# A hybrid diffusion step: the expert slot table from one-hot products, and adaLN products in column groups

## What is computed

```python
# adaLN: per layer, for the context and the latent conditioning
mod = silu(c) @ w_ada[l] + b_ada[l]            # 1024 x 6144 weights
sh1, sc1, g1, sh2, sc2, g2 = split(mod, 6)
h  = rmsnorm(x, norm_g[0]) * (1 + sc1) + sh1   # then h @ w_in, mixers, @ w_out
x  = x + g1 * mix
h2 = rmsnorm(x, norm_g[1]) * (1 + sc2) + sh2
x  = x + g2 * moe(h2)

# MoE: sigmoid router, the best 4 of 8 groups, the best 8 of 64 experts for each token
scores = sigmoid(h2 @ w_router)
gates  = 2.5 * chosen / sum(chosen)            # 8 for each token
routed = sum_e gates_e * (silu(h2 @ w_gate[e]) * (h2 @ w_up[e])) @ w_down[e]
shared = (silu(h2 @ ws_gate) * (h2 @ ws_up)) @ ws_down
```

## Time and profile before

| | us |
|---|---|
| median of 3 runs | 1783.19 |
| lowest and highest | 1767.92 to 1783.76 |
| the profiled execution, its own time | 1778.72 |
| its span in the trace | 1776.5 |
| mean granted TensorE clock | 0.901 |

### The profile page before, as it was taken

How to read it: one execution, slowest core, us unless ns; L and a number is a source line. 1 busy time by engine, 2 the same in 40 slices (tenths; PEclk the granted TensorE clock), 3 DMA queues, 4 the chain that set the end, 5 groups by cost and what they waited for, 6 DMA issues and landing times. The chain is left out here.

```text
span 1776.5 us, 23526 instructions
## 1 busy us (share of the span) xinstructions
PE 1466.6 (83%) x8676; PEld 945.6 (53%) x8676; DVE 670.5 (38%) x1341; ACT 422.5 (24%) x797; POOL 318.5 (18%) x351
## 2 busy tenths in 40 slices
PE   5899978991999999998079998799649999999952
PEld 2478563950555555554026975566425555555521
DVE  2623567153222222222644337633512222222246
ACT  2333515120122222221033344321102211221201
POOL 2000000005223232321110000000243223223220
PEclk9899959995899999999589998799869999999975
DMA  8644102224699988885855322122159888889844
GB/s 282 221 142 148 69 36 83 95 83 180 226 339 349 338 327 329 298 316 177 347 189 203 122 101 95 39 95 95 57 208 365 312 310 331 318 305 336 315 192 166
DMA packets 127760, 379.22 MB, mean 213 GB/s; under 512 B 29824, under 2 KB 34752, under 8 KB 124448
## 3 DMA queue, kind: packets, MB, share of 16 engines
q1 hardware_dynamic: 86976, 291.31, 44.6%
q0 software_dynamic: 40672, 86.42, 13.5%
HBM read 480.47 MB, written 64.91 MB: 307 GB/s over the span
## 5 line engine op out<-in xcount | busy, mean ns | idle before, releaser
L1171 PE MATMUL bank<-slab,xT 128*64 128x256 f32 x2112 | 300.3, 396 | 21.3 <-issue 20.8
L1171 PEld LDWEIGHTS bank<-slab,xT 128*64 128x64 f32 x2112 | 180.9, 142 | 103.4 <-issue 36.9
L744 POOL DMA_INDIRECT sums_scratch<-h,table x112 | 112.8, 1007 | 539.3 <-PE bank L1157 437.4
L1840 DVE TENSOR_TENSOR work<-work,bank 128x128 f32<-128x128 f32 x112 | 32.3, 288 | 408.6 <-ACT work L1437 408.6
L1171 PE MATMUL bank<-ring,xT 128*64 128x256 f32 x960 | 150.2, 389 | 12.0 <-issue 12.0
L1186 PE MATMUL bank<-slab,work 128*64 128x512 f32 x528 | 147.4, 592 | 1.5 <-DVE work L1844 1.5
L828 PE MATMUL bank<-ring,scond 128*2 128x512 f32 x320 | 140.9, 598 | 1.0 <-issue 1.0
L1437 ACT ACTIVATE work<-bank 128x128 f32<-128x128 f32 x112 | 31.0, 277 | 456.8 <-PE bank L1171 456.8
L1518 DVE TENSOR_TENSOR w_lo<-ring,w_hi 128x2048 fp32r<-128x2048 f32 x32 | 72.9, 2291 | 157.2 <-ACT w_hi L1259 157.0
L1157 PE MATMUL bank<-consts,big 128*128 128x128 f32 x544 | 77.8, 288 | 65.2 <-DMA big<-rows_scratch,table 65.2
L1829 DVE COPY h<-bank 128x512 f32<-128x512 f32 x112 | 77.5, 692 | 127.2 <-PE bank L1186 127.2
(11 more groups left out here) (336 smaller groups left out, 2376.7 us busy)
## 6 DMA issues: line engine op xcount, KB each, us to landing
slab<-in_w_gate SPq DMA_DIRECT2D x112, 512.0 KB
slab<-in_w_up SPq DMA_DIRECT2D x112, 512.0 KB
slab<-in_w_down SPq DMA_DIRECT2D x112, 512.0 KB
ring<-in_w_ada SPq DMA_DIRECT2D x24, 2048.0 KB
ring<-in_w_gate SPq DMA_DIRECT2D x52, 512.0 KB
ring<-in_w_up SPq DMA_DIRECT2D x52, 512.0 KB
ring<-in_w_down SPq DMA_DIRECT2D x52, 512.0 KB
slab<-sums_scratch POOLq DMA_DIRECT2D x24, 1024.0 KB, 11.2
```

The costliest lines, as they stand in the source:

```text
L744: pool.indirect_dma_start(sums_dram, bass.IndirectOffsetOnAxis(ap=table[:, u, 0:1], axis=0), y_rows[:, n % 3, :], None, bounds_check=TOK * ...
L1171: last = mm(bk[r, 0:2 * P].rearrange("p (k f) -> p k f", k=2), xT[:, n % 2, j, r], w[:, j, :, :], start=(j == 0), stop=(j == NJ - 1))
```

## The change

Three parts, and a few moves that go with them.

1. *The table.* Slots are numbered unit by unit (128 slots each) instead of slot by slot. A slot number is split into its unit and its place in the unit; VectorE compares both with a row of counting numbers, which gives one-hot matrices `of_slot` (128 places) and `of_unit` (56 units, times the result row less an empty mark), and 24 TensorE products of 128x128 by 128x56 add up the table in PSUM. VectorE adds the empty mark back, and a shift by three gives the token. The DRAM table, its early filling, the 24 scatters and the read back go.
2. *The order of the routing.* Only one shared product up stands in front of the counts; the other stands around the ranks, and the owner product comes before the shared down products. VectorE makes the owners as soon as the windows are known. The gates are worked out inside the units 4, 6 and 8. The twelve loads at a layer's end are issued from ScalarE's queue.
3. *adaLN.* All six modulations use one product: four feature chunks go to four column groups of 32 (`scond_wide` has two columns with data and 30 zeros), which leave four partial rows in one bank; the transposes are now of full 128 rows into two banks, and VectorE adds the four parts. The split of ada1 goes.

```diff
-        mod_rows = sb("mod_rows", [4, 2, D])
-        scond_r = sb("scond_r", [P, NJ, 4], F32R)
+        mod_rows = sb("mod_rows", [P, 2, D])
+        scond_wide = sb("scond_wide", [P, NJ, GROUP])
...
-        split_blocks = [b for b, (n, _) in enumerate(fixed) if n in ("ada1", "q", "k", "v", "fn+hq", "hif", "hbg")]
+        split_blocks = [b for b, (n, _) in enumerate(fixed) if n in ("q", "k", "v", "fn+hq", "hif", "hbg")]
...
-                pool.wait_ge(table_empty, 16 * (l + 1))
-                pool.wait_ge(slots_ready.sem, slots_ready.at(l, 1))
-                for k in range(NTILE * TOP_K):
-                    pool.indirect_dma_start(table_dram, bass.IndirectOffsetOnAxis(ap=slot_index[:, k:k + 1], axis=0),
-                                            row_ids[:, k, :], None).then_inc(dispatched, 16)
-                pool.wait_ge(dispatched, 16 * NTILE * TOP_K * (l + 1))
-                pool.dma_start(table[:, :, :].rearrange("p u c -> p (u c)"), table_dram.rearrange("(p u) c -> p (u c)", p=P))\
-                    .then_inc(table_in, 16)
-                pool.wait_ge(table_in, 16 * (l + 1))
+                pool.wait_ge(tokens_ready.sem, tokens_ready.at(l, 1))
...
+                def modulation_product(m, halves=(0, 1)):
...
-                        for ji in range(4):
-                            for c in range(2):
...
-                                last = mm(bk[0:2, :], scond[:, 4 * half + ji, :], w[:, ji, c * 512:(c + 1) * 512],
-                                          start=(half == 0 and ji == 0), stop=(half == 1 and ji == 3))
...
+                        for c in range(2):
...
+                            for ji in range(4):
+                                last = mm(bk[GROUP * ji:GROUP * (ji + 1), :], scond_wide[:, 4 * half + ji, :], w[:, ji, c * 512:(c + 1) * 512],
+                                          start=(half == 0), stop=(half == 1))
...
+                shared_up(0, range(NJ))
                 bk = banks.claim(pe, "places")
...
+                shared_up(1, range(0, 2))
                 bk = banks.claim(pe, "ranks")
...
+                shared_up(1, range(2, NJ))
+                bk = banks.claim(pe, "owner")
+                pe.wait_ge(windows_split.sem, windows_split.at(l, 1))
+                banks.filled(mm(bk[0:1, 0:E + NXW], expert_col[:, :], owner[0:E, :], start=True, stop=True), "owner")
...
+                bk = banks.claim(pe, "table")
+                for t in range(NTILE):
+                    pe.wait_ge(one_hots.sem, one_hots.at(l, t + 1))
+                    for k in range(TOP_K * t, TOP_K * (t + 1)):
+                        last = mm(bk[:, 0:NUNITS], of_slot[:, k, :], of_unit[:, k, :], start=(k == 0), stop=(k == NTILE * TOP_K - 1))
+                banks.filled(last, "table")
...
                 squares_of_x(x_ready.at(l, 0))
                 rows_of_modulation(0)
-                split(range(0, 2))
                 root_of_mean("ms1")
-                split(range(2, 4))
                 rows_of_modulation(1)
...
+                for i in range(3):
+                    act_e.wait_ge(y_kept[i], 16 * (l * uses_of(i) + uses_of(i)))
+                for m in range(4 * NTILE):
+                    if m >= 6:
+                        act_e.wait_ge(sums_used.sem, sums_used.at(l, m - 5))
+                    act_e.dma_start(sums_in[:, m % 6, :],
...
             def modulation(m):
...
+                for half in range(2):
+                    bk = banks.read(dve, f"modT{m}", half)
+                    parts = bk[:, :].rearrange("p (j g s) -> p j s g", j=4, g=4)[:, :, 0:2, :]
+                    banks.emptied(red(mod[:, m, 4 * half:4 * half + 4, :], parts, AX.X, ALU.add), f"modT{m}", half)
...
+                after(ts(slot_i[:, 0, :], slots, -1.0, None, ALU.add))
+                ts(slot_i[:, 1, :], slot_i[:, 0, :], P - 1, None, ALU.bitwise_and)
+                after(ts(slot_i[:, 2, :], slot_i[:, 0, :], 7, None, ALU.arith_shift_right))
+                after(copy(slot_f[:, :, :], slot_i[:, 1:3, :]))
...
+                    after(tt(of_unit[:, ks, :], window_ids[:, 0:NUNITS].unsqueeze(1).broadcast_to([P, TOP_K, NUNITS]),
+                             per_unit(slot_f[:, 1, ks]), ALU.is_equal))
+                    tt(of_slot[:, ks, :], window_ids[:, :].unsqueeze(1).broadcast_to([P, TOP_K, P]),
+                       slot_f[:, 0, ks].unsqueeze(2).broadcast_to([P, TOP_K, P]), ALU.is_equal)
+                    tt(of_unit[:, ks, :], of_unit[:, ks, :], per_unit(row_less_empty[:, ks]), ALU.mult).then_inc(one_hots.sem, 1)
...
+                banks.emptied(ts(row_table[:, :], bk[:, 0:NUNITS], float(EMPTY), None, ALU.add), "table")
+                banks.wait_emptied(dve, "table")
+                ts(token_table[:, :], row_table[:, :], 3, None, ALU.logical_shift_right).then_inc(tokens_ready.sem, 1)
...
+                    if n in (4, 6, 8):
+                        gates_matched((n - 4) // 2)
```

More of the change, by code:

```diff
@@ L377, in trunk_program @@
         banks.turn = 0
-        for stage, n in (("ada0", 2), ("ms1", 1), ("modT0", 1), ("ada1", 2), ("modT1", 1),
-                         ("ada2", 2), ("q", DH), ("k", DH), ("modT2", 1), ("v", NTILE), ("fn", NTILE), ("hq", 2),
+        for stage, n in (("ada0", 2), ("ms1", 1), ("modT0", 2), ("ada1", 2), ("modT1", 2),
+                         ("ada2", 2), ("q", DH), ("k", DH), ("modT2", 2), ("v", NTILE), ("fn", NTILE), ("hq", 2),
                          ("hif", NTILE), ("hbg", NTILE), ("k_rows", 1), ("ckT", 1), ("rotq", 2), ("rotk", 2),
@@ L412, in trunk_program @@
         banks.plan("layer", "owner", 1, [7])
+        banks.plan("layer", "table", 1, [6])
         for stage, b in (("XTa", 0), ("XTb", 1), ("GU", 2), ("AT", 3), ("Ya", 4), ("Yb", 5)):
@@ L1117, in _, with shared_up @@
                 pe.wait_ge(shared_in, 48 * (l + 1))
-                for k in range(2):
-                    bk = banks.claim(pe, "sh", k)
-                    for j in range(NJ):
+                def shared_up(k, tiles):
+                    bk = banks.claim(pe, "sh", k) if tiles[0] == 0 else banks.banks[banks.uses["layer"]["sh", k][0]]
+                    for j in tiles:
                         last = mm(bk[:, 0:TOK], w_shared[:, k * D + j * P:k * D + (j + 1) * P], h[:, j, :],
                                   start=(j == 0), stop=(j == NJ - 1))
-                    banks.filled(last, "sh", k)
+                    if tiles[-1] == NJ - 1:
+                        banks.filled(last, "sh", k)
+                shared_up(0, range(NJ))
                 bk = banks.claim(pe, "places")
                 pe.wait_ge(taken_ready.sem, taken_ready.at(l, 1))
+                for t in range(NTILE):
+                    mm(bk[:, NTILE * E:(NTILE + 1) * E], ones[:, :], taken[:, t, :], start=(t == 0), stop=(t == NTILE - 1))
+                for t in range(NTILE):
+                    mm(bk[0:E, (NTILE + 1) * E:(NTILE + 1) * E + 1], taken[:, t, :], ones[:, 0:1], start=(t == 0), stop=(t == NTILE - 1))
                 for t in range(NTILE):
@@ L1284, in _ @@
                 rows_of_modulation(2)
-                split(range(8, 10))
+                split(range(4, 6))
                 heads_out("k", kT)
-                split(range(10, 13))
+                split(range(6, 9))
                 for t in range(NTILE):
@@ L1290, in _ @@
                     banks.emptied(af(u_fn[:, t, :], bk[:, 0:FN], ACT.Copy), "fn", t)
-                split(range(13, 14))
+                split(range(9, 10))
                 for i in range(2):
@@ L1294, in _ @@
                     banks.emptied(af(hqT[:, i, :], bk[:, 0:TOK], ACT.Silu), "hq", i)
-                split(range(14, NUNIT))
+                split(range(10, NUNIT))
                 for t in range(NTILE):
@@ L1789, in _ @@
-                after(ts(own_place, own_place, 1.0, None, ALU.add))
+                banks.emptied(stt(place[:, :, :], count, 1.0, over_b[:, :, :], ALU.add, ALU.add), "places")
+                bk = banks.read(dve, "owner")
+                banks.emptied(ts(owner_i[:, :], bk[0:1, 0:E + NXW], float(NOBODY), None, ALU.add), "owner")
                 banks.wait_emptied(dve, "places")
```

214 lines of the change are left out of this document (85 added, 129 removed).

## The result

The changed kernel took 1699.48 us (median of 3 runs, 1698.66 to 1706.42), the kernel before 1783.19: a ratio of 0.9548, 95% interval 0.9458 to 0.9639 (ratios here are estimated from all runs, so they are not quite the quotients of the medians). Two more measurements of the changed kernel, with 4 and 6 runs, gave 0.9514 (0.9463 to 0.9564) and 0.9536 (0.9509 to 0.9563). The prediction was 1698.0.

What follows compares the result with a forecast made beforehand. It took TensorE to bound the expert units, and the slot table (36.7 us per layer) to delay them. Terms sum to -40.6 per layer, -81 in two, from 1778.72 to 1698 us; the forecast's own range is 1682 to 1715.

Steps and rivals of the forecast that it cites:

- The table and the owners: Router to first expert unit: table without scatters, earlier owners and weights; TensorE starts the units 22.5 us earlier per layer.
- The column groups run side by side: adaLN products: four column groups run together, one modulation's 32 instructions taking 4.0 us instead of 13.89.
- The start of a layer: ada0 and ada1, ahead of q: blocks read sooner, q starts 12.2 us earlier, less 1.8 for a cold start: -10.4 per layer.
- ada2's second half: Between q and k on a busy TensorE: product falls from 6.95 to 2.0 us, -4.7 per layer.
- ada3: Beside VectorE and ScalarE: VectorE's reading of the modulation grows from one small instruction to three, +0.5 us per layer.
- ada4 and ada5: Attention norm to router: ada4 gives -1.8 us per layer; ada5 0, router starting 2.3 earlier but cold, about 2.3 dearer.
- The rival of the clock: Projections after the layer's start stay at 1.2 GHz after TensorE idles: 75 us more per layer, 1848 in all; chance 0.03.
- The end of a layer: Sums loaded from ScalarE's queue, skipping GpSimd's issue of six: -1.7 us per layer as a mean of both layers.
- The gates inside the units: Units 4, 6 and 8: 2.1 us of VectorE work in each fits its free time, cost 0.
- The units bound by the weights: Rival, expert units: weights start only 14.8 us earlier, so 14.8 of 22.5 reaches the end, 1713; chance 0.11.
- No cold starts, quick gather: Rival: short bursts keep the clock and the first gather lands in 4.2 us, giving 1681; chance 0.14.

Runs made afterwards that it cites:

- the busy router: Changed kernel plus 9 overwritten 128x256 products between ada5's halves and 7 more between ada5 and the router: 1687.48 us, ratio 0.9489 to the kernel before.

## Why the prediction was right, step by step

- *The table and the owners, -22.5.* Right in mechanism and, once the router's loss is taken apart, in size. First gather at 403.76, 48.6 behind the router's start, 68.1 before: 19.5 earlier against the router, where the prediction's sign was about 25. It landed after 6.9 us (6.7 expected); one-hots 7.1 us (7.7), table products 5.46 (5.6). The stage as a whole is 17.5 shorter. The router's loss in it is 4.3 (9.9 on average over the six layers seen, 5.57 before) and that of the transposes of h 1.2 (4.0 and 2.79), so 23.0 without them; with the busy router, where both are measured away, the stage takes 49.7, 22.3 less than before. Scatters back cost 32.6 by the rest of the span, 42.3 by the medians; the forecast has 45 for the two layers, the earlier weights and owners with them.
- *The column groups run side by side.* Right: 3.64 us, 4.0 expected. The Trainium skill (TensorE: Matmul & The Clock Gate, Measured speedup vs the span model) has 2.38 times for three column groups; the runs here have 13.92 / 7.06 = 1.97 for two and 13.92 / 3.64 = 3.8 for four, near the ideal, and the measurement decides.
- *The start of a layer, -10.4.* Right in layer 0: q's weights asked for at 46.23 (47), q at 62.32 (61.6). In layer 1 q gained 9.4 instead of 12.2 at its start; why it gained less is not shown.
- *ada2's second half, -4.7, and ada3, +0.5.* Right: with q's cold start of 1.8 behind q's start, -2.9 was predicted from q to ada3 and -3.1 measured; ada3 to ada4 +0.5 and +0.5.
- *ada4 and ada5, -1.8 and 0.* Here a size was off, twice. The router starts 5.7 earlier, not 4.1: 3.4 come from ada4 up to the output projection (1.8 predicted), 2.3 from ada5, as predicted. And "cold, about 2.3 dearer" is the step that failed: I took a cold start for a fixed price of 1.7 to 2.0 us, read from the earlier trace rows and the shared down products. It isn't fixed. Where TensorE had idled 1.4 to 2.5 us for VectorE's h, and some 4 us within ada5 before that, the router took 8.7 to 10.5 us instead of 5.57, most or all of it at half speed, and the transposes behind it lost about 1 more. That makes about 5 us in place of 2.3, and ada5's term a loss of about 3 in place of 0. The Trainium skill (TensorE: Matmul & The Clock Gate, Loop structure matters more than you think) has this rule, that matmuls behind a wait for a DMA run cold; I let it bear on the projections alone and priced it by one burst that had paid 1.65 of its 15.54 us. The router paid 3.2 to 4.9 on a burst of 5.57; the busy router, which pays nothing, and the kernels with one and two groups, whose longer ada5 leaves no such idle time, show that the idle time was the cause.
- *The rival of the clock.* It put the loss at the projections. q ran at half speed from 62.32 for about 4.6 us and at full speed behind that (0.98 of the full clock from 62.3 to 190.3), so its 75 us per layer never came; the loss was at the router.
- *The end of a layer, -1.7.* Too much: 0.3. On either queue the first sum waits for the last y copy: VectorE's wait is 16.13 us, 16.16 in the earlier trace rows.
- *The gates inside the units, 0.* No run has the gates alone. Nothing speaks against it: the unit stage is no longer than before.
- *The units bound by the weights.* If the stops once in seven units are waits for weights, it is half right as a fact, but they are there before the change too; it takes nothing of the 22.5.
- *No cold starts, quick gather.* Neither half came: the router paid for its idle time, and the gather landed in 6.4 to 7.4, not 4.2.

The total came out within 2 us of the median because the steps that gave more (ada4 to router, the units' shorter stages, 1.6 and 3.2 per layer) and those that gave less (router to units 2.7, start 1.7, layer's end 1.4) offset each other. That it is so close is luck: eight of the changed kernel's thirteen timed runs lie more than 2 us from 1698, and the forecast takes its 81 from the profiled 1778.72, while the medians shown differ by 83.7. The sum is shown to that extent only; the 3.2 of the units is within their spread.

## What to carry to other kernels

A table of indices that is built by tens of small scatters costs their issue, one after the other (24 of 1.3 us here); one-hot products build it on TensorE in 5.5 us, and 7 of VectorE. A faster product ahead of a wait takes the work away that kept TensorE's clock up, and what follows pays: price the next burst at half speed over its whole length if it is as short as the router's (5.57 us), and fill the wait with products that are overwritten, up to close before the burst: 5.0 us too early did nothing for q. Where one stage makes the spread between runs, compare profiles without that stage.

## What the runs showed of the hardware

- One, two and four column groups of 32 columns (fp32, 128x512): 13.92, 7.06, 3.64 us for the same 32 instructions. Little is lost up to four (13.92 / 4 = 3.48).
- The granted clock follows what TensorE did just before: 1.00 instead of 0.78 in the same stretch, by products that compute nothing that is used.
- Behind stops of 1.4 to 3.9 us in the units the same 32 instructions take 3.67 us in some executions and 5.0 to 6.7 in others; over 28 unit stages the granted clock goes from 1.00 (382.0 us) to 0.96 (394.9).
- The first gather of token rows lands 4.0 to 4.5 us after its issue where no weights move or the last load is held back, and 6.4 to 8.2 among weight loads.
